# A norm by tokens and value tiles ahead of the convolution at the beginning, and the stick-breaking stage in a new order

## The chip, the core and the metric

The kernel runs on one core of one Trainium2 chip. A core has TensorE (PE, matrix multiply, results go to eight banks of PSUM), VectorE (DVE), ScalarE (ACT), GpSimd (POOL) and SyncE (SP), each with its own instruction queue, worked off in order; they wait for each other by semaphores. The metric is the device time of one execution in microseconds (us). Before the change it is 1169.18 us, the median of three runs (1169.01 to 1170.82).

## What is computed

Two transformer blocks on x of 256 tokens by 1024 features, in float32. The change touches only the mixer of the first block:

```python
h = rms_norm(x, norm_mix_g[l])
p = h @ w_in[l]
q = rms_norm(p[..., :s1].reshape(bsz, L, SB_HEADS, SB_HEAD_DIM), sb_q_norm_g[l])
k = rms_norm(p[..., s1:s2].reshape(bsz, L, SB_HEADS, SB_HEAD_DIM), sb_k_norm_g[l])
v = p[..., s2:s3].reshape(bsz, L, SB_HEADS, SB_HEAD_DIM)
o_sb = stick_breaking_attention(q, k, v)
o_conv = conformer_conv(p[..., s3:s4], ...)     # 31 taps, layer norm, silu, 256x256 matrix
o_ssm = s5_ssm(p[..., s4:], ...)                # 16 groups, 64 complex states, gated output
mixed = jnp.concatenate([rms_norm(o_sb, ...), rms_norm(o_conv, ...), rms_norm(o_ssm, ...)], axis=-1)
x = x + mixed @ w_out[l]
hx = rms_norm(x, norm_xa_g[l])
hm = rms_norm(mem, norm_mem_g[l])
x = x + memory_cross_attention(hx, hm, ...)     # keys and values of mem: hm @ xa_wk, hm @ xa_wv
```

In stick-breaking attention (8 heads of 64) a weight is exp(log_sigmoid(z) + the sum of log_sigmoid(-z) over the keys that come later). Behind this come cross attention, a gated feed-forward layer, and a second block of two layers with three more attentions and two feed-forward layers; none of it is changed.

## The kernel before

**Tiles and pieces.** Activations lie with features on the 128 partitions: a tile is 128 features by 256 tokens, and x is eight of them (xT). Weights come in pieces of 1 MB (1024 rows by 256 columns) into three slots `raw`. Each piece is split in halves: ScalarE copies a half to `whi` in a rounded format, VectorE writes raw minus whi to `wlo` (`split`). Activations are split likewise (act_hi, act_lo; mem_hi, mem_lo in mem_pair). A projection tile is 24 matmuls, three for each of eight row blocks: whi by act_hi, whi by act_lo, wlo by act_hi (lines 2009 to 2011; 2074 to 2076 with tokens as output rows for values). A slot's next piece may be split once the tiles of the old one are done: `after(name, idx)` stands on ScalarE and VectorE where the splits are due, and SP loads a piece when the low parts of the slot's last one are written.

**Order.** All orders are written by hand, one program for each engine; `Plan` only numbers tiles, pieces, PSUM banks (a ring of four) and semaphore values. The order on TensorE: 16 transposes of x, 16 of mem, sums of squares of x by matmuls with ones (`norm_sums`), transposes of the row vectors (gains, convolution taps: `col`, `tap`), the two tiles u (input of the state-space branch), with the sums of squares of mem between them, cb and ca (gate and input of the convolution, two tiles each), then q and k in turn (four each) with `ssm_matrices` and the first `conv_taps` among them, value tiles v with `inputs_of(1)` and `conv_sum` among them, and the stick-breaking stage.

**Stick-breaking stage.** For each of 8 heads: `scores_of(h)` (one head ahead), ScalarE's `sb_log1p` (three steps), VectorE's `sb_softplus`, `sums_of(h)` (matmuls with a triangle), ScalarE's Exp, `values_of(h)`. Between them TensorE does the 16 tiles of cross attention's keys (xk) and values (xv), two for each head (`kv_tile`), and small work for the other branches (`side_work`). In heads 0 to 3 the state-space branch runs along: `inputs_of(s)` writes one pair of state inputs to PSUM, ScalarE copies it to SBUF (`bu_out`, line 924), VectorE works a quarter of the states (`state_quarter`, 13 operations), `outputs_of(q)` reads them. The norms of the three branches, ("branch", 1) of the convolution, ("branch", 2) of the state-space branch and ("branch", 0) of stick-breaking, come at the end, and then `branch_projection` with w_out.

The generic helper lines: 766 is ScalarE's split, 1360 VectorE's, 2080 a plain matmul, 1353 a VectorE product, 1371 the scaling by a norm, 790 squares, 835 and 837 the logarithm and exponential of a norm.

## Time and profile before

| | us |
|---|---|
| median of three runs | 1169.18 |
| the profiled execution | 1177.42 |
| its span | 1175.3 |
| TensorE, VectorE, ScalarE, GpSimd busy | 1118.8, 839.6, 618.3, 39.2 |
| x landed, first matmul of u | 7.7, 25.3 |
| end of the second u tile | 39.3 |
| first matmul of q, of v | 55.1, 100.2 |
| taps of the convolution, two parts | 78.3 to 85.4, 92.1 to 100.3 |
| first scores, first value tile of mem | 120.0, 193.2 |
| end of the last value tile of mem | 234.1 |
| first matmul of xq, behind w_out | 269.6 |

A page of the profile gives each engine's busy time and what ended its idle time; the queries on the trace give the same for any stretch.
### The profile page before, as it was taken

Reading aid. Unit: us, or ns where it says so; the run is one execution under the profiler, and the core shown is the slowest. Engines: PE = TensorE matmul, PEld = TensorE weight load, DVE = VectorE, ACT = ScalarE, POOL = GpSimd, SP = SyncE. Lnnn points to the kernel's source line nnn. Section 1 sums busy time; section 2 is a strip of 40 time slices with the busy share of each in tenths; the row PEclk is TensorE's granted clock in tenths of the full one; section 3 lists DMA queues with packets and bytes.
Section 4 is the critical chain, followed back from the end, with each engine's and each line's share of the span. In section 5 each row is a group of like instructions: output and inputs, shape, how many; then the busy total and the mean of one; then the engine's idle time right before and its main releaser. Section 6 shows DMA issues by size and latency. Waiting matters only on the chain.

```text
span 1175.3 us, 20129 instructions
## 1 busy us (share of the span) xinstructions
PE 1118.8 (95%) x7660; PEld 988.1 (84%) x7660; DVE 839.6 (71%) x1277; ACT 618.3 (53%) x1104; POOL 39.2 (3%) x41
## 2 busy tenths in 40 slices
PE   5899899989999999999999999999999999999997
PEld 4787678879998999999987698999998779888886
DVE  2785686246678787887556678787887877788885
ACT  4634344556555554556355555454556675455554
POOL 2000000001020000001000010000001001000000
PEclk8998889989999999999999999999999999999999
DMA  8342312325366765655531056665758235576661
GB/s 265 109 144 73 108 37 73 108 70 164 90 192 178 214 178 164 193 176 172 165 126 36 1 180 180 205 176 158 211 143 186 66 91 177 145 214 186 181 169 72
DMA packets 218431, 169.69 MB, mean 144 GB/s; under 512 B 20827, under 2 KB 208130, under 8 KB 218242
## 3 DMA queue, kind: packets, MB, share of 16 engines
q1 hardware_dynamic: 217106, 164.44, 48.0%
q0 software_dynamic: 640, 2.95, 0.7%
q10 hardware_dynamic: 624, 1.44, 0.4%
q8 instruction: 44, 0.72, 0.3%
q14 instruction: 17, 0.14, 0.0%
HBM read 167.76 MB, written 1.05 MB: 144 GB/s over the span
## 4 chain that ended last, share of the span: by engine, by line
PE 80%; DVE 9%; ACT 7%; issue 2%; SPq 1%; DMA 1%; POOLq 0%; POOL 0%; DVEq 0%; ACTq 0%
PE bank L2441 19%; PE bank L2080 17%; PE bank L2009 10%; PE bank L2443 10%; PE bank L2010 9%; PE bank L2011 9%; DVE wlo L1360 2%; DVE arena L1353 2%; PE bank L2074 2%; PE bank L2076 2%; PE bank L2075 2%; ACT whi L766 1%; SPq L691 1%; ACT arena L1303 1%; DVE wlo L1756 1%
## 5 line engine op out<-in xcount | busy, mean ns | idle before, releaser
L2441 PE MATMUL bank<-mem_pair,whi 128*128 128x512 f32 x1056 | 375.8, 399 | 0.7 <-DVE xT L1677 0.7
L2443 PE MATMUL bank<-mem_pair,wlo 128*128 128x256 f32 x1056 | 296.3, 281 | 0.0
L2441 PEld LDWEIGHTS bank<-mem_pair,whi 128*128 128x128 f32 x1056 | 198.5, 188 | 47.7 <-issue 0.9
L1360 DVE TENSOR_TENSOR wlo<-raw,whi 128x1024 fp32r<-128x1024 f32 (+3 forms) x137 | 161.5, 1223 | 97.2 <-ACT whi L766 96.2
L2009 PE MATMUL bank<-act_hi,whi 128*128 128x256 f32 (+1 forms) x744 | 216.5, 291 | 10.5 <-DVE act_lo L1379 4.7
L2010 PE MATMUL bank<-act_lo,whi 128*128 128x256 f32 (+1 forms) x744 | 212.9, 286 | 0.0
L2011 PE MATMUL bank<-act_hi,wlo 128*128 128x256 f32 (+1 forms) x744 | 212.8, 286 | 0.0
L1756 DVE TENSOR_TENSOR wlo<-raw,whi 128x1024 fp32r<-128x1024 f32 x177 | 208.9, 1221 | 5.3 <-ACT whi L1140 1.6
L2443 PEld LDWEIGHTS bank<-mem_pair,wlo 128*128 128x128 f32 x1056 | 199.5, 189 | 0.8
L1140 ACT ACTIVATE whi<-raw 128x1024 fp32r<-128x1024 f32 x180 | 179.7, 1045 | 0.3 <-PE bank L2080 0.3
L2009 PEld LDWEIGHTS bank<-act_hi,whi 128*128 128x128 f32 (+1 forms) x744 | 143.8, 193 | 20.5 <-issue 13.2
L1160 ACT ACTIVATE arena<-arena 128x256 f32<-128x256 f32 x66 | 27.6, 418 | 249.4 <-DVE arena L1353 249.4
L2010 PEld LDWEIGHTS bank<-act_lo,whi 128*128 128x128 f32 (+1 forms) x744 | 144.0, 193 | 0.8 <-issue 0.7
L2011 PEld LDWEIGHTS bank<-act_hi,wlo 128*128 128x128 f32 (+1 forms) x744 | 144.0, 194 | 0.0
L2080 PE MATMUL bank<-arena 32*32 32x256 f32 (+9 forms) x1052 | 132.8, 384 | 8.7 <-ACT arena L924 2.1
L766 ACT ACTIVATE whi<-raw 128x1024 fp32r<-128x1024 f32 (+3 forms) x134 | 129.2, 1018 | 18.1 <-PE bank L2011 18.1
L1786 DVE TENSOR_REDUCE arena<-bank 128x256 f32<-128x512 f32 x132 | 90.7, 687 | 64.9 <-PE bank L2443 64.9
L1353 DVE TENSOR_TENSOR arena<-arena 128x256 f32<-128x256 f32 (+5 forms) x190 | 95.3, 503 | 40.5 <-ACT arena L1164 21.3
L2080 PEld LDWEIGHTS bank<-arena 32*32 32x32 f32 (+5 forms) x1052 | 81.6, 135 | 45.0 <-issue 14.9
L2009 PE MATMUL bank<-mem_pair,whi 128*128 128x256 f32 (+1 forms) x352 | 107.5, 305 | 2.1 <-DVE mem_pair L1670 2.1
L2010 PE MATMUL bank<-mem_pair,whi 128*128 128x256 f32 (+1 forms) x352 | 101.8, 289 | 0.0
L2011 PE MATMUL bank<-mem_pair,wlo 128*128 128x256 f32 (+1 forms) x352 | 101.5, 288 | 0.0
(221 smaller groups left out, 1442.9 us busy)
## 6 DMA issues: line engine op xcount, KB each, us to landing
raw<-in_ffn_w_in_dram SPq DMA_DIRECT2D x132, 512.0 KB, 5.2
raw<-in_ffn_w_out_dram SPq DMA_DIRECT2D x33, 1024.0 KB, 5.1
raw<-in_w_in_ab_dram SPq DMA_DIRECT2D x11, 1024.0 KB, 6.2
raw<-in_w_in_dram SPq DMA_DIRECT2D x9, 1024.0 KB, 7.0
raw<-in_xa_wk_dram SPq DMA_DIRECT2D x4, 1024.0 KB, 5.5
raw<-in_xa_wv_dram SPq DMA_DIRECT2D x4, 1024.0 KB, 5.0
raw<-in_w_out_dram SPq DMA_DIRECT2D x4, 1024.0 KB, 5.1
raw<-in_xa_wq_dram SPq DMA_DIRECT2D x4, 1024.0 KB, 5.1
```

The costliest lines, as they stand in the source:

```text
L766: act.activation(whi[g % SLOTS][:, h * n:h * n + n], raw[g % SLOTS][:, h * n:h * n + n], ACT.Copy)\
L1140: act.activation(whi[slot][:, h * 1024:h * 1024 + 1024], raw[slot][:, h * 1024:h * 1024 + 1024], ACT.Copy).then_inc(s_split_hi, 1)
L1353: return dve.tensor_tensor(dst, a, b, ALU.mult)
L1360: dve.tensor_tensor(wlo[g % SLOTS][:, at_], raw[g % SLOTS][:, at_], whi[g % SLOTS][:, at_].bitcast(F32), ALU.subtract).then_inc(s_split_lo, 1)
L1756: dve.tensor_tensor(wlo[slot][:, at_], raw[slot][:, at_], whi[slot][:, at_].bitcast(F32), ALU.subtract)\
L1786: dve.tensor_reduce(x[:, j, :], bank[2 * j + g][:].rearrange("p (h t) -> p t h", h=2), AX.X, ALU.add)\
L2009: pe.matmul(dst, w[0], a[0], start=start, stop=False, **kw)
L2010: pe.matmul(dst, w[0], a[1], start=False, stop=False, **kw)
L2011: return pe.matmul(dst, w[1], a[0], start=False, stop=stop, **kw)
L2080: return pe.matmul(dst, w, a, start=start, stop=stop, skip_group_check=True)
L2441: pe.matmul(b[:].rearrange("p (h t) -> p h t", h=2), w[0][:, k, g, :], mem_pair[:, :, k, :], start=k == 0, stop=False, skip_group_check=True)
L2443: last = pe.matmul(b[:, 0:T], w[1][:, k, g, :], mem_hi[:, k, :], start=False, stop=k == KC - 1, skip_group_check=True)
```

## The change

**Beginning.** The norm of x and of mem is taken token by token before the transposes. x lands in two halves (128 tokens each, tokens on partitions); ScalarE squares a half with a running sum for each token (`token_scale`), takes Ln and Exp of two columns, and ScalarE and VectorE scale one half each. TensorE transposes the scaled tokens, and ScalarE (`normed_high`) and VectorE (`normed_low`) write the high and low parts straight from PSUM with the gain. x is also transposed unscaled, for the residual; VectorE copies it out (`raw_out`). The gain of this norm and the 128x128 identity get loads of their own. The two u tiles are computed together, row block by row block. The three first weight pieces go to SP's queue before the row vectors, and mem is loaded by GpSimd, once piece u has landed. `token_transposes` of mem stand behind tile (cb, 1) and behind ca. 16 ones-matmuls go, 17 transposes come.

**q, k, v and the convolution.** All value tiles stand ahead of `conv_taps(0)`, and the taps, inputs_of(0), inputs_of(1) and conv_sum stand in one block before the first scores. VectorE's qk_norm, coefficients and rotations are spread anew to fit.

**Stick-breaking stage.** Scores run two heads ahead. softplus(0) stands inside the first state quarter. On TensorE outputs_of(h) stands between the two inputs of the next states, with scores_of(h + 2) ahead of both. ScalarE's splits are moved behind a head's weights, half by half (`kv_split`). The norm of the convolution and of the state-space branch is a slot earlier each; the squares of the stick-breaking outputs come in three parts, the last straight from PSUM, and the first four tiles of w_out take their conv rows, then their state-space rows, then the stick-breaking rows.

TensorE at the start of the program, before: x_landed and mem_landed are the two loads, ones the matrix of the sums.

```order
L2119 MATMUL bank<-cst,arena 128x128 [waits x_landed,consts_landed]
L2119 MATMUL bank<-cst,arena 128x128 x15
L2126 MATMUL bank<-cst,arena 128x128 [waits mem_landed]
L2126 MATMUL bank<-cst,arena 128x128 x15
L2080 MATMUL bank<-sq,ones 128x256 [waits squares_ready,transposes_evacuated,pool_step]
L2080 MATMUL bank<-sq,ones 128x256
L2080 MATMUL bank<-sq,ones 128x256 [waits squares_ready]
L2080 MATMUL bank<-sq,ones 128x256
L2080 MATMUL bank<-sq,ones 128x256 [waits squares_ready]
```

The same place after, up to the first row block of u (x_scaled lies in hf and sq, the unscaled x in arena):

```order
L2208 MATMUL bank<-cst,arena 128x8 [waits mix_gain_landed,identity_landed]
L2212 MATMUL bank<-cst,arena 128x128 [waits x_landed0]
L2212 MATMUL bank<-cst,arena 128x128 x7
L2212 MATMUL bank<-cst,arena 128x128 [waits x_landed1]
L2212 MATMUL bank<-cst,arena 128x128 x7
L2202 MATMUL bank<-cst,hf 128x128 [waits tokens_scaled1,tokens_scaled0,transposes_evacuated]
L2202 MATMUL bank<-cst,sq 128x128
L2202 MATMUL bank<-cst,hf 128x128
L2202 MATMUL bank<-cst,sq 128x128
```

mem and the sums of squares are gone from the head of TensorE's queue. ScalarE after, from the last high copies of x's norm to the copies of col and tap:

```order
L873 ACTIVATE act_hi<-bank,mix_gain 128x256 x4
L783 ACTIVATE whi<-raw 128x1024 x4
L860 ACTIVATE rms,tok_sums<-arena 128x1024
L860 ACTIVATE arena,tok_sums<-arena 128x1024
L863 ACTIVATE tok_scale<-tok_sums,eps 128x2
L866 ACTIVATE tok_scale<-tok_scale 128x2
L910 ACTIVATE arena<-arena,tok_scale 128x1024
L798 ACTIVATE arena<-bank 128x256 x2
L783 ACTIVATE whi<-raw 128x1024 x2
L914 ACTIVATE col<-bank 128x109
L915 ACTIVATE tap<-bank 128x62
L918 ACTIVATE arena<-log_dt 64x8 x2
```

In before the same queue had col and tap ahead of the first high copies:

```order
L766 ACTIVATE whi<-raw 128x1024 x2
L835 ACTIVATE rms<-bank,eps 128x256
L837 ACTIVATE rms<-rms 128x256
L869 ACTIVATE col<-bank 128x109
L870 ACTIVATE tap<-bank 128x62
L844 ACTIVATE act_hi<-hf 128x512 x4
L766 ACTIVATE whi<-raw 128x1024 x4
L790 ACTIVATE sq<-bank 128x512 x4
```

So col and tap moved behind the splits of three pieces, mem's squares and u's evacuation; TensorE's tile (cb, 1) waits for them as before.

TensorE behind the values of head 1 up to the first key tile of head 2, before (sq,ones is the squares' sum, 32x256 outputs, 128x256 inputs and scores):

```order
L2080 MATMUL bank<-sq,ones 128x256 [waits rms_ready,squares_ready,bu_evacuated]
L2080 MATMUL bank<-sq,ones 128x256
L2080 MATMUL bank<-arena 32x256 [waits sb_out_evacuated,states_ready]
L2080 MATMUL bank<-arena 32x256 x7
L2080 MATMUL bank<-arena 128x256 [waits bu_evacuated,rms_ready]
L2080 MATMUL bank<-arena 128x256
L2080 MATMUL bank<-arena 128x256 [waits bu_evacuated]
L2080 MATMUL bank<-arena 128x256
L2080 MATMUL bank<-arena 128x256 [waits sb_weights,tile_evacuated_dve]
L2080 MATMUL bank<-arena 128x128
L2080 MATMUL bank<-cst 128x128 x2
```

After:

```order
L2161 MATMUL bank<-sq,ones 128x256 [waits rms_ready,squares_ready,bu_evacuated]
L2161 MATMUL bank<-sq,ones 128x256
L2161 MATMUL bank<-arena 128x256 [waits sb_weights,tile_evacuated_dve]
L2161 MATMUL bank<-arena 128x128
L2161 MATMUL bank<-cst 128x128 x2
L2161 MATMUL bank<-arena 128x256 [waits bu_evacuated,rms_ready]
L2161 MATMUL bank<-arena 128x256
L2161 MATMUL bank<-arena 32x256 [waits sb_out_evacuated,states_ready]
L2161 MATMUL bank<-arena 32x256 x7
L2161 MATMUL bank<-arena 128x256 [waits bu_evacuated]
L2161 MATMUL bank<-arena 128x256
```

The scores stand first now, and the outputs between the two inputs.

The core of the diff:

```diff
-    sp.dma_start(x_tok, ins["x"][0].rearrange("(t p) d -> p t d", p=P)).then_inc(s_x, 16)
-    load(pieces[0])
-    for name, k in VECTORS:
+    for t in range(TT):
+        sp.dma_start(x_tok[:, t, :], ins["x"][0, t * P:t * P + P, :]).then_inc(s_x[t], 16)
+    for g in range(SLOTS):
+        load(pieces[g])
+    for name, k in VECTORS[1:]:
...
+    pool.wait_ge(s_landed[0], 16)
+    pool.dma_start(m_tok, ins["mem"][0].rearrange("(t p) d -> p t d", p=P)).then_inc(s_mem, 16)
...
+    def token_scale(which, tok, landed):
+        for t in range(TT):
+            act.wait_ge(*landed[t])
+            act.activation((rms, v_sb)[t].rearrange("p a n -> p (a n)"), tok[:, t, :], ACT.Square,
+                           accum_out=tok_sums[:, which, t:t + 1]).then_inc(s_toksq, 1)
+        act.wait_ge(s_toksq, 2 * which + 2)
+        act.activation(tok_scale[:, which, :], tok_sums[:, which, :], ACT.Ln, scale=1.0 / D, bias=eps[:, 0:1])\
+           .then_inc(s_tokln, 1)
+        act.wait_ge(s_tokln, which + 1)
+        act.activation(tok_scale[:, which, :], tok_scale[:, which, :], ACT.Exp, scale=-0.5).then_inc(s_tokr, 1)
+        act.wait_ge(s_tokr, which + 1)
+    def normed_high(which, c):
+        hi, gain = (act_hi, mem_hi)[which], (mix_gain, col[:, ROW["norm_mem_g"]:ROW["norm_mem_g"] + KC])[which]
+        act.wait_ge(s_tr, (TR_X, TR_MEM)[which] + c + 1)
+        act.activation(hi[:, c, :], bank[4 + c % 4][:, (c // 4) * T:(c // 4) * T + T], ACT.Copy,
+                       scale=gain[:, c:c + 1]).then_inc(s_nhi, 1)
...
+    act.activation(mix_gain[:], bank[4][:, 0:KC], ACT.Copy).then_inc(s_trev, 1)
+    token_scale(0, x_tok, [(s_x[t], 16) for t in range(TT)])
+    act.activation(sq.rearrange("p a n -> p (a n)"), x_tok[:, 1, :], ACT.Copy, scale=tok_scale[:, 0, 1:2])\
+       .then_inc(s_tok[1], 1)
+    act.wait_ge(s_trev, 1)
+    for h in range(2):
+        split(0, h)
+        for c in range(4 * h, 4 * h + 4):
+            normed_high(0, c)
...
+    token_scale(1, m_tok, [(s_mem, 16)] * TT)
+    act.activation(m_tok[:, 1, :], m_tok[:, 1, :], ACT.Copy, scale=tok_scale[:, 1, 1:2]).then_inc(s_tok[1], 1)
+    for i in range(2):
+        evacuate("u", i, u[:, i, :])
+    act.wait_ge(s_tr, TR_ROWS + 1)
+    act.activation(col[:], bank[3][:, 0:ROWS], ACT.Copy).then_inc(s_trev, 1)
+    act.activation(tap[:], bank[3][:, T:T + 62], ACT.Copy).then_inc(s_trev, 1)
...
+    for h in range(4):
+        kv_tile(2 * h)
+        sb_weights(h)
+        kv_tile(2 * h + 1)
+        kv_split(h, 0)
+        if h % 2:
+            sb_out(h)
+        rms_of(("xk", h), bank[4][:, 0:T], 256)
+        kv_split(h, 1)
+        if h < 3:
+            bu_out(2 * h + 2)
+        sb_log1p(h + 2)
+        if h < 3:
+            bu_out(2 * h + 3)
...
+    sb_weights(7)
+    branch_high(0)
+    squares(("branch", 0), 1, o_sb[:, 2, :], T)
+    branch_high(1)
+    kv_tile(15)
+    act.wait_ge(s_sbo, 8)
+    squares(("branch", 0), 2, bank[7][:, 0:T], T)
+    sb_out(7)
+    rms_of(("branch", 0), bank[4][:, 0:T], 512)
+    kv_split(7, 0)
+    branch_high(2)
+    branch_high(3)
+    kv_split(7, 1)
...
+    raw_out(0)
+    raw_out(1)
+    dve.wait_ge(s_tokr, 1)
+    dve.tensor_scalar(hf.rearrange("p a n -> p (a n)"), x_tok[:, 0, :], tok_scale[:, 0, 0:1], None, ALU.mult)\
+       .then_inc(s_tok[0], 1)
+    for h in range(2):
+        split(0, h)
+        for c in range(4 * h, 4 * h + 4):
+            normed_low(0, c)
+    raw_out(2)
+    raw_out(3)
...
+    state_quarter(0, lambda: sb_softplus(0))
+    sb_softplus(1)
...
+    pe.wait_ge(s_raw, 2)
+    for c in range(KC):
+        if c % 4 == 0:
+            pe.wait_ge(s_split_lo, split_value(0, c // 4))
+        pe.wait_ge(s_nlo, c + 1)
+        w = [x[:, c, :] for x in weights(("w_in", "u", 0))]
+        for i in range(2):
+            last = three(ring_bank("u", i)[:, 0:T], [x[:, P * i:P * i + P] for x in w],
+                         (act_hi[:, c, :], act_lo[:, c, :]), c == 0, c == KC - 1)
+            if c == KC - 1:
+                last.then_inc(tile_done, 1)
+        if c < 4:
+            token_transposes(x_scaled, 0, (c + 4,))
...
         project("k", j, ("w_in", "k", j // 2), P * (j % 2))
-        if j == 1:
-            ssm_matrices()
-        if j >= 2:
-            conv_taps(j - 2)
-        if j == 3:
-            inputs_of(0)
     for i in range(4):
         project_tokens("v", i, ("w_in", "v", i // 2), i % 2)
         if i == 0:
             sum_squares(("qk", 3), 0, bank[4][:], 2, True, True, blocks)
-            inputs_of(1)
-            conv_sum()
+        if i == 1:
+            ssm_matrices()
+    conv_taps(0)
+    conv_taps(1)
+    inputs_of(0)
+    inputs_of(1)
+    conv_sum()
...
+    scores_of(1)
+    pe.wait_ge(s_nlo, 2 * KC)
     for h in range(8):
-        if h < 7:
-            scores_of(h + 1)
-        if h == 0:
-            pe.wait_ge(s_h, HF["norm", 1] + 4)
         kv_tile(2 * h)
         side_work(h, SLOT_A)
         sums_of(h)
...
             if h:
                 pe.wait_ge(s_bu_ev, 2 * h + 2)
             sum_squares(("xk", h), 0, bank[4][:, 0:T], 2, True, True)
-            outputs_of(h)
+        if h < 6:
+            scores_of(h + 2)
         if h < 3:
             pe.wait_ge(s_rms, 2 * stat_no["xk", h] + 1)
             inputs_of(2 * h + 2)
+        if h < 4:
+            outputs_of(h)
+        if h < 3:
             inputs_of(2 * h + 3)
-    sum_squares(("branch", 2), 0, bank[4][:, 0:T], 2, True, True)
-    pe.wait_ge(s_sbev, 4)
-    sum_squares(("branch", 0), 0, bank[7][:, 0:T], 2, True, False)
-    sum_squares(("branch", 0), 1, bank[7][:, 0:T], 2, False, True)
+    sum_squares(("branch", 0), 0, bank[4][:, 0:T], 2, True, False)
+    sum_squares(("branch", 0), 1, bank[4][:, 0:T], 1, False, False)
...
+        for m0, parts in ((0, ((4, 5), (6, 7), (0, 1, 2, 3))), (4, ((4, 5, 6, 7, 0, 1, 2, 3),))):
+            for part, order in enumerate(parts):
                 for m in range(m0, m0 + 4):
                     b = claim("w_out", m, ("w_out", m // 2)) if part == 0 else ring_bank("w_out", m)
                     w = [x[:, :, P * (m % 2):P * (m % 2) + P] for x in weights(("w_out", m // 2))]
-                    for i, k in enumerate(order):
-                        if m == 0 and i % 2 == 0:
-                            pe.wait_ge(s_h, HF["branch", 0] + 2 * part + i // 2 + 1)
+                    for k in order:
+                        if m == 0 and k % 2 == 0:
+                            pe.wait_ge(s_h, HF["branch", 0] + (2 + k // 2 if k < 4 else k // 2 - 2) + 1)
                         last = three(b[:, 0:T], [x[:, k, :] for x in w], [x[:, k, :] for x in hi_lo],
-                                     part == 0 and i == 0, part == 1 and i == 3)
-                    if part:
+                                     k == 4, k == 3)
+                    if part == len(parts) - 1:
                         last.then_inc(tile_done, 1)
+                    if m == 0 and part == 0:
+                        sum_squares(("branch", 0), 2, bank[4][:, 0:T], 1, False, True)
```

## Rows read from the trace of the kernel before

**Rows 1.** The page: busy time and share of the span, by engine.

```profile
PE 1118.8 (95%) x7660; PEld 988.1 (84%) x7660; DVE 839.6 (71%) x1277; ACT 618.3 (53%) x1104; POOL 39.2 (3%) x41
```

**Rows 2.** Six stages: stretch, length, busy us (instructions) by engine, PEclk, DMA, GB/s.

```profile
0.00:25.30 25.30, 11.15 (x50) 9.38 (x50) 4.70 (x8) 10.38 (x17) 6.24 (x15) 0.91 0.91 280
25.30:55.10 29.80, 24.08 (x161) 22.71 (x161) 22.59 (x54) 17.83 (x31) 0.00 (x0) 0.90 0.41 131
55.10:120.00 64.90, 61.58 (x810) 53.08 (x810) 45.21 (x69) 26.74 (x43) 0.00 (x0) 0.92 0.32 102
120.00:193.10 73.10, 64.29 (x384) 52.07 (x384) 53.95 (x78) 29.61 (x54) 0.00 (x0) 0.88 0.21 70
193.10:234.00 40.90, 39.45 (x280) 36.16 (x279) 12.95 (x19) 20.75 (x38) 0.00 (x0) 1.00 0.31 103
234.00:270.00 36.00, 31.49 (x217) 29.42 (x216) 19.27 (x32) 18.02 (x31) 2.60 (x2) 0.91 0.26 86
```

**Rows 3.** TensorE's waits, 0 to 270 us: us in total, times, longest.

```profile
PE bank L2080 <- DVE arena L1578: 5.0, 1, 5.0
...
PE bank L2009 <- DVE act_lo L1379: 4.7, 2, 2.9
PE bank L2009 <- ACT arena L908: 4.3, 1, 4.3
PE bank L2080 <- ACT arena L924: 2.1, 3, 0.7
```

**Rows 4.** Timeline of the beginning: start, us, engine, line, operation.

```profile
7.71 3.41 PE L2119 MATMUL bank<-cst,arena 128*128 128x128 f32 x16 [7.71 <-DMA arena<-in_x_dram]
...
21.96 0.32 PE L2133 MATMUL bank<-cst,arena 109*128 109x109 f32 x1 [1.70 <-DMA arena<-in_ssm_lam_im_dram]
...
25.34 0.55 PE L2009 MATMUL bank<-act_hi,whi 128*128 128x256 f32 x1 [2.87 <-DVE act_lo L1379]
```

**Rows 5.** DMA issues, 0 to 60 us: KB each, us from issue to landing.

```profile
arena<-in_x_dram SPq DMA_DIRECT2D x1, 1024.0 KB, 6.8
...
arena<-in_ssm_glu_w_dram POOLq DMA_DIRECT2D x1, 512.0 KB, 8.8
```

**Rows 6.** Tile raw, 0 to 2 us: the load of the first weight piece.

```profile
DMA to landing us min/median/max: 16.0/16.0/16.0
```

**Rows 7.** Timeline of ScalarE: two high copies of a weight piece.

```profile
39.74 2.01 ACT L766 ACTIVATE whi<-raw 128x1024 fp32r<-128x1024 f32 x2
```

**Rows 8.** Timeline of VectorE: four low parts of weights, four scaled mem tiles.

```profile
29.27 4.63 DVE L1360 TENSOR_TENSOR wlo<-raw,whi 128x1024 fp32r<-128x1024 f32 x4 [0.25 <-ACT whi L766]
...
45.58 1.65 DVE L1371 SCALAR_TENSOR_TENSOR hf<-bank,col,rms 128x256 f32<-128x256 f32 x4
```

**Rows 9.** Four stretches, columns as in rows 2.

```profile
130.00:140.00 10.00, 9.06 (x44) 7.83 (x46) 2.25 (x4) 2.75 (x5) 0.00 (x0) 0.66 0.32 107
140.00:170.00 30.00, 27.75 (x158) 22.52 (x155) 22.13 (x33) 11.12 (x23) 0.00 (x0) 0.83 0.21 71
145.00:150.00 5.00, 5.00 (x22) 4.60 (x21) 4.57 (x7) 1.74 (x4) 0.00 (x0) 0.50 0.15 54
250.00:260.00 10.00, 10.00 (x86) 10.00 (x85) 3.40 (x5) 3.44 (x5) 0.00 (x0) 1.00 0.00 0
```

**Rows 10.** Timelines of TensorE and VectorE, one head of the stick-breaking stage.

```profile
174.35 2.98 PE L2080 MATMUL bank<-arena 128*32 128x256 f32 x20
...
179.80 1.42 DVE L1353 TENSOR_TENSOR arena<-arena 128x512 f32<-128x512 f32 x2 [2.53 <-ACT arena L924]
...
189.98 0.84 PE L2080 MATMUL bank<-arena 128*32 128x256 f32 x6 [0.88 <-DVE arena L1353]
```

**Rows 11.** Timeline of TensorE behind the last value tile.

```profile
237.75 1.13 PE L2080 MATMUL bank<-sq,ones 128*128 128x256 f32 x4 [2.04 <-ACT sq L790]
...
245.66 0.39 PE L2009 MATMUL bank<-act_hi,whi 128*128 128x256 f32 x1 [1.82 <-DVE act_lo L1379]
```

456 lines of the change are left out of this document (226 added, 230 removed).

## The prediction

> **What bounds the kernel now.** I read the page's totals first, then TensorE's waits, then a table by stages, then the timelines of the stages where the waits sit. TensorE is busy 95% of the span and VectorE 71% [rows 1], so a gain can only come from where TensorE stands still or runs at the lower of its two clock levels. The table by stages covers the part that the change touches, up to 270 us, where the first tile of the next projection begins; after it nothing is changed [rows 2]. There TensorE is busy 11.2 of 25.3, 24.1 of 29.8, 61.6 of 64.9, 64.3 of 73.1, 39.5 of 40.9 and 31.5 of 36.0 us: 38.0 us idle in all. The granted clocks of the same rows (0.91, 0.90, 0.92, 0.88, 1.00, 0.91) are means over 1.0 and 0.5, the levels of 2.4 and 1.2 GHz. Length times what is missing to 1.0 is the time lost: 2.3 + 3.0 + 5.2 + 8.8 + 0 + 3.2 = 22.5 us. So 60.5 us of these 270 are not matmul work at full rate. The longest waits: 7.7 for x [rows 4], and [rows 3] 5.0 on softplus (L1578), 4.7 on the low halves act_lo, 4.3 on the sigmoid's exponential (L908), 2.1 on the state inputs' copies (L924).
>
> **Beginning: from the start to the first q tile (before: 55.1 us).** In before, x lands at 7.7; all transposes of x and mem, squares, ones-matmuls and the row vectors (wait until 21.96 for ssm_lam_im) come ahead of the first projection, at 25.34, and it starts at half rate [rows 4]. After: x comes in two halves, alone at the head of its queue, the identity apart. The old x took 6.8 us to land with the constants beside it [rows 5]; I put the first half at 5.2 and the second at 6.7. Sixteen transposes took 3.41 us [rows 4], so they end near 8.7. ScalarE's squares (1024 columns, 1.0 us each by the weight copies [rows 7]), Ln, Exp and the scaled copy end near 9.8; eight scaled transposes follow, half of 3.41, 1.7 us. Piece u now travels right behind x, so not 16.0 us after issue [rows 6] but at about 10. Copy to whi 1.0, low part 1.2 [rows 7, 8], first low activation 0.4 (four in 1.65 [rows 8]): u's matmuls begin at 12.6. 48 matmuls and four pairs of transposes take 5.8 + 0.9 us at full rate (86 matmul records in 10 us near 250 [rows 9], a few missing, so 0.12 each and 2.9 a tile); the first half of them at half rate makes it end near 20.5. In before both u tiles were done at about 39.
>
> Then comes the new wait. Tile (cb, 1) needs col and tap, and on ScalarE these stand behind the four copies of pieces cb and ca (3.9), two squares of mem (2.1), Ln and Exp (0.5), one scaled copy (1.05), two evacuations (0.66), two copies of the q piece (2.0) and themselves (0.45): 10.7 us behind the last high activation, at about 18, plus some 1.3 for landings: 30. Tile (cb, 0) runs 22.6 to 25.5, so TensorE waits about 4.6 us here, and such a wait (5.0 us, before the sums of head 0) left it at half rate for most of the next 10 us (0.66 [rows 9]: 3.4 us lost), here I take 1.7 us. Then cb1 and the two ca tiles, 8.9, and sixteen mem transposes at full rate, half of 3.41 or 1.8, plus the 1.7: q starts at 42.5 to 43 instead of 55.1. The half-rate slice at 55 goes too. **Term A: -13.5.** Bounds: -5, if the third piece or mem lands 6 us later and pushes ScalarE's whole row of work; -17 without the wait. VectorE's chain (low halves, 5.5 us of phase arithmetic, low activations) ends near 50, ahead of q1's statistics; ScalarE is back from its two table loads at 49, just before it is needed at 51.
>
> **Value tiles ahead of the convolution.** No matmul goes or comes; the order changes, so that the 15 us of taps and the state inputs come last and what VectorE prepares for them (diagonals, matrices, rotations) has 15 us more. The 65 us held 3.3 idle and 5.2 of lost clock [rows 2]. The rotations, six operations of 1.2 us a half, end near 97 in my count, when the taps end: a tie. I take -5 and leave the rest for a half-rate slice where TensorE hangs on ScalarE's copies between the last tap and the first scores. **Term B: -5**, bounds +2 and -8.5.
>
> **Head 0 of the stick-breaking stage.** In before softplus(0) stood on VectorE behind the whole first state quarter (13 operations, 10.2 us) and two low halves; TensorE waited 5.0 us [rows 3] and lost 3.4 us of clock after it [rows 9]. Now it stands after the quarter's fifth operation, 3.6 us in, and TensorE has two score groups and a tile (5.8 us) to do. Covered by 1.5 us. **Term C: -8.4**, bounds -4 (another wait of a few us) and -8.4.
>
> **Heads 1 to 3.** One head from outputs to outputs is 174.35 to 189.98, 15.6 us [rows 10], with a wait for a copy of the state inputs (2.1 in three [rows 3], 0.7 each) and 0.88 for the states. Now scores and outputs lie between the two state inputs, so the copy is hidden. But the loop outputs, second input, copy, ten us of states, outputs is a closed one: 2.1 + 0.9 + 0.7 + 10.15 (179.80 to 189.95, its first two operations and the release of the outputs stand in [rows 10]) = 13.9, beside TensorE's own work of 14.07. A tie again; from 15.6 to 14.3 three times. **Term D: -4**, bounds 0 and -9 (the half rate between 140 and 170, clock 0.83, 5.1 us lost [rows 9], gone too). I keep it.
>
> **Tail, after the last value tile.** Before: 1.45 us idle in the fifth stage and 4.5 in the sixth, 2.04 and 1.82 of these before the branch sums and before the stick-breaking rows [rows 11], as the norms of three branches follow each other, and 3.2 us of lost clock [rows 2]: 9.2 together. After: two norms are done before tile 15, the squares of the last pair are split off, and 48 matmuls on the conv and ssm rows (5.8 us) stand between the last squares and the first use of the stick-breaking rows, whose chain I make 0.4 + 0.4 + 0.8 + 0.9 + 1.0 + 0.6 + 0.7 = 4.8 us. Covered. **Term E: -9**, bounds -5 and -9.2.
>
> **Sum.** -13.5 - 5 - 8.4 - 4 - 9 = -39.9. Nearly every term assumes that the next item is ready with 0 to 1.5 us to spare in four places (rotations, states, q and k norms twice), and each miss costs a wait and perhaps a half-rate slice of 1.7 us. I add 4.9 for these: -35. The profiled execution took 1177.4 us, 2.1 more than its span, and 8.2 more than the median 1169.2; the sum is a difference of two executions of one kind, so it is taken from the median: 1134.
>
> **A rule against the sum.** Half rate stands at 145 to 150 us, where TensorE is busy 5.00 of 5.00 us [rows 9] and the longest wait shortly before is 0.7 us. The Trainium skill (TensorE: Matmul & The Clock Gate, HAM oscillation) has the clock fall at pauses for data. By that rule, with the long waits gone, the half rate of heads 1 to 3 would go as well, and the sum would be 5 us better; the row speaks against it, and I go by the row.
>
> **Rivals.** (1) *The beginning shifts its bound to ScalarE.* Its list behind u has no gap, so any late landing goes straight to cb1. For it: in before the first piece needed 16.0 us against 6.8 for x of the same size [rows 5, 6], since 4 KB rows of mem went beside 1 KB rows of weights; now three pieces, mem and the small tensors still share the engines. Price: A -7.5, D -1, two more half-rate slices: -22, 1147. (2) *All waits and all half-rate slices go:* A -15, B -8, C -8.4, D -6, E -9: -46.4, less a rest of 1.4: -45, 1124. Against it: half rate without long waits [rows 9]. (3) *Only one of the two parts pays,* the other being eaten by a VectorE chain (rotations late by 7 us in front of the state copies): -12, 1157. (4) *Slower.* mem is now asked for by GpSimd, only after piece u. The largest transfer that GpSimd issued in before, 512 KB, landed 8.8 us after its issue [rows 5]. ScalarE and TensorE stand behind it. Everything else pays some 35 us, so mem would have to be usable at 18 + 35 = 53 us or later instead of 18 to have the kernel no faster; at 60 it would be 7 us slower, 1176. Nothing in the trace is near it. (5) The waits are replaced one for one: no change.
>
> The Trainium skill (DMA: Bandwidth & Descriptors, Queues, rings and completion order) says that each engine takes turns between queue rows by whole packets; by it mem, in long rows, takes more than its share beside the third piece, in short ones. The 16.0 us of the first piece agree [rows 6]; what it does here is the condition of rival 1.
>
> **Chances.** Forecast 45%, rival 1 25%, rival 2 18%, rival 3 7%, no change 2%, rival 4 3%. The forecast alone spans 1128 to 1141. The range for 8 in 10 reaches to rival 2 and most of rival 1: 1121 to 1152. 0.2% is 2.3 us, about what a measurement tells from nothing: faster 95%, same 2%, slower 3%.
>
> **What would show it.** Right: u's matmuls from about 12 to 21 us; one wait of 3 to 6 us before cb1, released by ScalarE's tap; q0 near 43; first scores near 101; no wait over 1 us on softplus; heads 14 to 14.5 us apart, half rate at one or two places among them; w_out from the last value tile on without a wait over 1 us; the first tile of the next projection near 232 instead of 269.6. Wrong: first u matmuls after 18 us, a wait of ScalarE on mem over 3 us, waits of TensorE on rotations or states of several us, or half-rate slices summing over 15 us.

## The result

The changed kernel takes 1133.1 us (median of four executions, 1132.4 to 1134.0) against 1170.0 for the kernel before (1169.0 to 1179.0). The ratio is 0.967, 95% interval 0.962 to 0.972. 1134 was predicted, with 1121 to 1152 as the range. In the profiled executions the span went from 1175.3 to 1130.9 us. These 44.4 us are more than the 36.9 between the medians, and the difference turns out to be the instructive part of this case.

The page after: busy time and share of the span, answering to [rows 1].

```profile
PE 1098.0 (97%) x7645; PEld 971.9 (86%) x7645; DVE 837.4 (74%) x1275; ACT 619.0 (55%) x1112; POOL 40.1 (4%) x42
```

All of TensorE's waits after, from the start to the first tile of the next projection at 224.95 us (us in total, times, longest), answering to [rows 3].

```profile
PE bank L2208 <- DMA cst<-consts_dram: 6.2, 1, 6.2
PE bank L2238 <- DMA arena<-in_ssm_lam_im_dram: 3.7, 1, 3.7
PE bank L2090 <- DVE act_lo L1459: 1.5, 1, 1.5
PE bank L2161 <- issue: 1.2, 1, 1.2
PE bank L2202 <- DVE hf L1471: 0.8, 1, 0.8
PE bank L2161 <- DVE arena L1420: 0.7, 1, 0.7
```

The reader is to see that softplus, the sigmoid, the copies of the state inputs and the squares have all gone from the list. What is left is the landing of the identity (x is no longer the last to land), one wait of 3.7 us for the row vectors, and four short ones.

Timeline of TensorE after, at the ends of the stages (start, us, engine, line, operation, idle time before it), answering to [rows 4, 10]: first transpose, first matmul of u, row vectors, first q tile, state inputs, first scores, last head with states, first tile of the value projection on mem, first tile of the next projection.

```profile
6.18 0.27 PE L2208 MATMUL bank<-cst,arena 8*128 8x8 f32 x1 [6.18 <-DMA cst<-consts_dram]
...
14.28 0.55 PE L2090 MATMUL bank<-act_hi,whi 128*128 128x256 f32 x1 [1.48 <-DVE act_lo L1459]
...
26.70 0.41 PE L2238 MATMUL bank<-cst,arena 109*128 109x109 f32 x1 [3.75 <-DMA arena<-in_ssm_lam_im_dram]
...
42.64 0.36 PE L2090 MATMUL bank<-act_hi,whi 128*128 128x256 f32 x1
...
96.42 2.87 PE L2161 MATMUL bank<-arena 32*32 32x256 f32 x28 [1.22 <-issue]
...
100.28 0.48 PE L2161 MATMUL bank<-arena 64*128 64x256 f32 x1
...
156.34 1.92 PE L2161 MATMUL bank<-arena 128*32 128x256 f32 x16 [0.70 <-DVE arena L1420]
158.19 0.39 PE L2155 MATMUL bank<-whi,mem_pair 128*128 128x256 f32 x1
...
224.95 0.28 PE L2090 MATMUL bank<-mem_pair,whi 128*128 128x256 f32 x1
```

The same stages by busy time, after (columns as in [rows 2]); the last row is the stretch behind the wait for the row vectors.

```profile
0.00:42.64 42.64, 30.42 (x196) 29.18 (x196) 22.29 (x40) 27.39 (x51) 7.12 (x16) 0.92 0.82 260
42.64:100.28 57.64, 56.42 (x814) 48.73 (x812) 49.71 (x90) 29.42 (x48) 0.00 (x0) 1.00 0.44 145
100.28:158.19 57.91, 57.21 (x385) 45.50 (x384) 51.90 (x76) 29.82 (x56) 0.00 (x0) 1.00 0.17 56
158.19:224.95 66.76, 66.76 (x491) 62.47 (x489) 32.46 (x52) 37.38 (x67) 2.59 (x2) 1.00 0.33 107
25.00:32.00 7.00, 5.30 (x24) 5.02 (x25) 4.68 (x5) 6.22 (x15) 0.00 (x0) 0.51 1.07 343
```

From 158.19 us on TensorE is busy 66.76 of 66.76 us. The clock is 1.00 (2.4 GHz) in three of four stages; the 0.92 of the first is the one stretch at 25 to 32 us at half rate (1.2 GHz). By its length it costs 3.4 us, and 2.6 of these while TensorE worked (busy 5.30 of 7.00 us), as it began inside the wait of 3.7. The rest of the program, 906 us from there, took the same time in both profiled executions.

```profile
14.28:18.30 4.02, 4.02 (x19) 4.02 (x20) 2.65 (x5) 1.30 (x3) 3.39 (x6) 1.00 1.07 372
18.42:22.96 4.54, 4.54 (x39) 4.33 (x37) 3.29 (x6) 3.43 (x6) 0.00 (x0) 1.00 1.06 260
```

19 matmuls in 4.0 us and 39 in 4.5: TensorE is at half rate up to 18.3 us. In the kernel before the record begins at 10.7 us, in its second profiled execution (below) at 16.8. So a clock row of the first stage is not to be compared between executions, and the mean clock of a whole execution is a little too high by an amount that varies.

### The profile page after: what moved, and what is told of

It reads as the page before. It is cut to its first block, busy times and chain, and to the rows that moved or that the text cites. A ratio compares the mean times of both kernels' runs of the same rounds, so it can differ in the third digit from the quotient of the medians.

```text
span 1130.9 us, 20116 instructions
## 1 busy us (share of the span) xinstructions
PE 1098.0 (97%) x7645; PEld 971.9 (86%) x7645; DVE 837.4 (74%) x1275; ACT 619.0 (55%) x1112; POOL 40.1 (4%) x42
## 4 chain that ended last, share of the span: by engine, by line
PE 86%; DVE 5%; ACT 5%; SPq 1%; issue 1%; DMA 1%; POOLq 0%; POOL 0%; DVEq 0%; ACTq 0%
PE bank L2542 20%; PE bank L2161 18%; PE bank L2090 11%; PE bank L2092 10%; PE bank L2091 10%; PE bank L2544 10%; PE bank L2155 2%; PE bank L2156 2%; PE bank L2157 2%; DVE wlo L1427 1%; DVE arena L1420 1%; ACT arena L1370 1%; DVE wlo L1837 1%; SPq L702 1%; DMA arena<-in_ssm_lam_im_dram 1%
## 5 line engine op out<-in xcount | busy, mean ns | idle before, releaser
L2092 PEld LDWEIGHTS bank<-act_hi,wlo 128*128 128x128 f32 (+1 forms) x744 | 143.2, 192 | 0.0
L1420 DVE TENSOR_TENSOR arena<-arena 128x256 f32<-128x256 f32 (+5 forms) x190 | 95.4, 504 | 32.7 <-ACT arena L1231 21.3
L2090 PE MATMUL bank<-mem_pair,whi 128*128 128x256 f32 (+1 forms) x352 | 105.1, 299 | 2.2 <-DVE mem_pair L1751 2.2
L2091 PE MATMUL bank<-mem_pair,whi 128*128 128x256 f32 (+1 forms) x352 | 99.5, 283 | 0.0
```

What stands on the lines that cost most here:

```text
L1420: return dve.tensor_tensor(dst, a, b, ALU.mult)
L2090: pe.matmul(dst, w[0], a[0], start=start, stop=False, **kw)
L2091: pe.matmul(dst, w[0], a[1], start=False, stop=False, **kw)
L2092: return pe.matmul(dst, w[1], a[0], start=False, stop=stop, **kw)
```

## The experiments

Twelve runs were made, in four groups, two of them repeats of before and after. The medians of the kernel before in the four groups were 1170.8, 1172.2, 1172.1 and 1172.1 us, and 1169.3 in the first experiment, since its executions spread over 10 us; so the kernels are compared with each other by their own medians, and the ratio to before stands beside where it matters.

**1. The kernel before, again.** No edit.

> The kernel before, once more. In the trace of before the span was 1175.3 us at a mean granted clock of 0.979, and its time 1177.4, 8.2 above the median of the other runs; the changed kernel's profiled execution agreed with its own median (1132.8 and 1133.1). Theory A (the clock makes the difference: in an ordinary run of before some of the half-rate slices of the trace are missing): runs of 1169 to 1171 us show a mean clock near 0.986, since 8.2 us of 1175 at half rate less is 0.007; runs near 1178 show 0.979; and a trace taken in a run of 1170 us lacks half rate at 140 to 170 us, where the trace of before lost 5.1 us, and part of another slice. Theory B (recording itself slows before): every recorded span is near 1175 us, whatever the clock.

Twelve executions: median 1169.3, from 1169.1 to 1176.0 us. Theory A held. The times of this kernel stand in steps, and the longer ones go with a lower clock (time, mean granted clock over the span; seven of the executions of before in this group):

```
1169.15  0.987      1174.45  0.982      1177.5   0.979
1170.78  0.987      1175.76  0.982      1179.01  0.979
1172.39  0.985
```

The profiled execution this time took 1169.2 us, span 1167.1. Its stages, cut at the same events as those of the changed kernel (first q tile, first scores, first value tile on mem, first tile of the next projection):

```profile
0.00:55.07 55.07, 35.38 (x210) 32.37 (x211) 27.29 (x61) 28.21 (x48) 6.24 (x15) 0.93 0.65 199
55.07:117.17 62.10, 59.40 (x811) 52.05 (x811) 45.24 (x69) 26.77 (x43) 0.00 (x0) 0.95 0.33 106
117.17:188.18 71.01, 62.19 (x386) 50.36 (x385) 54.56 (x79) 29.62 (x54) 0.00 (x0) 0.90 0.23 75
188.18:261.51 73.33, 67.60 (x492) 62.26 (x490) 31.05 (x48) 38.79 (x69) 2.41 (x2) 1.00 0.29 95
```

TensorE waits as in the first trace of before (5.0 for softplus, 4.3 for the sigmoid; idle 36.9 us up to here and 38.0 there), but the clock's records hold only 13.6 us lost up to here, and 22.2 in the first. The first stage tells nothing of this: its record starts later here, and it is 55.1 us long in both. From the first q tile on the three stages are 206.4 us long and 214.5 in the first trace. Of these 8.1 us, 0.9 are idle time and 7.2 are clock (9.9 us lost for 17.1): half rate is missing at 239 to 250 us, and there is less of it from 140 to 170. The same program, the same waits, another 8.1 us: this is the 8.2 us by which the first profiled execution lay above the median. Which stretches of this program fall to half rate is not the same from one execution to the next.

The mean clock orders the times of this kernel, but not of every one. The beginning alone (experiment 2) took 1152.4 us at a mean clock of 0.983 and 1155.2 at 0.988, softplus(0) put back (experiment 3) 1138.1 at 0.989 and 1139.6 at 0.994. Only one execution of each was traced, so why is not shown.

**2. Each part alone.** The diffs are the two halves of the change: the beginning with value tiles ahead of the convolution, and the order of heads and tail. (Where they meet, the sum of squares of the stick-breaking branch has two groups in the first and three in the second.)

> Only the new beginning (norm by tokens, value tiles ahead of the convolution); the stick-breaking stage in its old order. Theory A (the two parts add, each by the terms of the prediction): -18.5 us (A -13.5, B -5), 1151. By the distances in the two traces it would be -19.8 (first q tile 55.1 to 42.6, first scores another 7.3 earlier), 1150. Rival (only the stick-breaking stage pays, since the rotations of VectorE now stand late, in front of the old order's first state quarter): -10 or less. The wait before the sums of head 0 should be back, 4 to 6 us, with half rate behind it.

> Only the new order of the stick-breaking stage; the old beginning. Theory A (prediction's terms C, D, E, -8.4 -4 -9): -21.4, 1148. Theory B (by the traces, where these stretches became 24.9 us shorter, less the 8.2 us by which the profiled run of before lay above its median, if those 8.2 lay in this stage): -16.7, 1153. Rival: -25 or more, if the two parts get in each other's way in the changed kernel, so that each alone gives more than its share of the 37. Heads 0 to 3 should stand 14.0 to 14.5 us apart with no wait over 1 us, and no half rate between 120 and 234 us if half rate only follows waits.

The beginning alone: 1154.0 us (1149.8 to 1155.3), 16.8 below before's 1170.8, ratio 0.983. The stick-breaking stage alone: 1150.9 (1149.5 to 1153.9), 19.9 below, ratio 0.981. Together 36.7; from the same 1170.8 the whole change gives 37.7 (36.9 from the 1170.0 of its own group). So the parts add to 1 us, or to 2.5 if the 1169.3 of experiment 1 is taken for before, and each lies near its terms (-18.5 and -21.4). Both pay, so the rival in which one eats the other is out.

One detail was not as expected. With the beginning alone, the wait for softplus(0) did not come back. TensorE ran at half rate from 98 to 109 us, through the scores and the first key tile:

```profile
98.00:109.00 11.00, 11.00 (x37) 7.88 (x36) 8.95 (x13) 5.09 (x10) 0.00 (x0) 0.53 0.01 1
```

It arrived at the sums at 110.3 us, and softplus(0) had just ended at 110.2. A slow stretch had taken the place of the wait. In the kernel with the new stick-breaking order alone there is no wait but one of 0.7 us from 117 to 234 us, and no half rate in it.

**3. Softplus(0), in before and in the changed kernel.** First the edit in before:

```
-            state_quarter(0)
+            state_quarter(0, lambda: sb_softplus(0))
...
-            sb_softplus(0)
```

> The kernel before, with one edit: softplus(0) stands behind the fifth operation of the first state quarter instead of behind the whole quarter. Theory A (term C): the wait of 5.0 us before the sums of head 0 goes, and the half rate directly behind it (3.4 us): -8.4, 1161. Theory B (half rate at 140 to 170 us is an after-effect of the same wait): the trace loses these 5.1 us as well, and against a profiled run of before -13.5; against ordinary runs, if those lack the half rate at 140 to 170, -5 to -8. Theory C (half rate at 145 to 150 us has nothing to do with that wait): the trace still shows a slice at half rate between 140 and 170 us.

1167.0 us (1164.4 to 1170.0), ratio 0.995, interval 0.993 to 0.997: 2.3 us below the twelve executions of experiment 1 (the two spans, 1164.8 and 1167.1, give the same), and not 8.4. The wait of 5.0 is gone. The heads give 0.9 of it back: a further wait for the exponential of the weights (L1030), perhaps as the loop of states now bounds them. And the clock gives nothing: 13.7 us lost as before. Half rate moved from 126 to 133 us to 133 to 140, where the waits ahead are short, and a stretch at 235 to 239 us makes the tail 1.5 us longer than in experiment 1:

```profile
120.00:133.00 13.00, 12.31 (x86) 9.55 (x84) 12.04 (x17) 6.58 (x13) 0.00 (x0) 1.00 0.14 43
133.00:140.00 7.00, 7.00 (x31) 6.59 (x31) 6.50 (x11) 2.14 (x4) 0.00 (x0) 0.51 0.67 222
```

Theory C: the half rate of the heads does not need the long wait. Then the same thing undone in the changed kernel:

```
-            state_quarter(0, lambda: sb_softplus(0))
+            state_quarter(0)
+            sb_softplus(0)
```

> The changed kernel with one edit undone: softplus(0) again behind the whole first state quarter. By the trace of the changed kernel the quarter then ends near 110.0 us, and TensorE stands ready for the sums of head 0 at 106.0: a wait of 4.5 us. Theory A (a pause of 5 us is what brings the half rate, term C): +4.5 and 3.4 us of half rate behind it, +7.9, 1141. Theory B (the half rate of before hangs on the many short waits, one or two of 0.7 to 0.9 us in each head, not on the one long wait; the previous run, in which this wait alone was taken from before, lost 13.7 us of clock as before did, 13.6): +4.5 and no half rate between 100 and 225 us, 1137.5. Rival (VectorE's loop of states gives the wait back in the later heads): +2 or less.

1138.7 us (1137.2 to 1139.9), 5.6 above the changed kernel. The timeline of TensorE and the stretch around it:

```profile
109.89 0.79 PE L2162 MATMUL bank<-arena,cst 128*128 128x256 f32 x1 [4.47 <-DVE arena L1650]
```

```profile
109.00:113.00 4.00, 3.11 (x13) 2.93 (x14) 1.30 (x3) 0.49 (x1) 0.00 (x0) 0.57 0.00 0
113.00:225.00 112.00, 111.30 (x778) 95.81 (x777) 70.32 (x104) 60.60 (x109) 1.30 (x1) 1.00 0.25 85
```

The 4.5 us are as worked out from the trace, and 1.7 us of clock go with them, half of Theory A's 3.4 and not the nothing of Theory B; behind them none. So this edit is worth 5.6 us in the changed kernel and 2 to 4 in before: what a wait costs depends on what stands around it.

**4. The order inside heads 0 to 2, undone.**

```
-                sb_log1p(h + 2)
-                if h < 3:
                     bu_out(2 * h + 3)
+                sb_log1p(h + 2)
...
-                if h < 6:
-                    scores_of(h + 2)
-                if h < 3:
-                    pe.wait_ge(s_rms, 2 * stat_no["xk", h] + 1)
-                    inputs_of(2 * h + 2)
                 if h < 4:
...
                 if h < 3:
+                    pe.wait_ge(s_rms, 2 * stat_no["xk", h] + 1)
+                    inputs_of(2 * h + 2)
                     inputs_of(2 * h + 3)
+                if h < 6:
+                    scores_of(h + 2)
```

> The changed kernel with the order inside heads 0 to 2 as before: outputs, both state inputs, then scores, and on ScalarE the two copies of the state inputs one behind the other, ahead of the scores' log1p. Theory A (term D, -4): the wait for the copy comes back, 0.7 us in each of three heads, and 0.9 for the states or the scores: heads 15.6 instead of 14.1 us apart, +4 to +5, 1137.5. Theory B (half rate follows such repeated short waits): besides, half rate at one to three places between 110 and 170 us, 1.7 to 5 us, so +6 to +10, 1141. Rival (no difference, since VectorE's loop of states bounds the heads in either order): +1 or less.

1139.3 us (1137.3 to 1141.8), 6.2 above the changed kernel. Rows of TensorE's timeline, then the stretches between:

```profile
115.19 0.48 PE L2160 MATMUL bank<-arena 32*128 32x256 f32 x1 [0.69 <-ACT arena L953]
...
131.42 0.69 PE L2160 MATMUL bank<-arena 32*128 32x256 f32 x2 [0.69 <-ACT arena L953]
...
147.61 0.69 PE L2160 MATMUL bank<-arena 32*128 32x256 f32 x2 [0.69 <-ACT arena L953]
```

```profile
116.00:120.00 4.00, 4.00 (x17) 3.35 (x16) 2.88 (x5) 1.68 (x4) 0.00 (x0) 0.57 0.73 257
120.00:133.00 13.00, 12.31 (x83) 9.51 (x82) 10.80 (x16) 5.79 (x11) 0.00 (x0) 1.00 0.06 20
133.00:137.00 4.00, 4.00 (x21) 3.87 (x20) 3.62 (x6) 1.72 (x4) 0.00 (x0) 0.57 0.59 202
```

The three waits of 0.69 us are back, and behind two of them TensorE runs at half rate while it is busy 4.00 of 4.00 us, 3.4 us lost in this execution. So Theory B. Idle time grew by 2.3 us (the 0.9 for the states stands where the changed kernel has 0.7), the clock's loss by 3.4. These 5.7 are more than this execution shows: at 1137.3 us it is the fastest of the six and 4.5 above the profiled one of the changed kernel, so not all of the half rate turned into time. The other five have a mean clock of 0.988 to 0.992 for its 0.993; they were not traced.

The other four traces with the old order bear it out. With this one they are five; each has the wait of 0.69 us three times, and in each half rate begins behind two of the three (us):

```
                    waits of 0.69 end at      half rate begins at
before              143.2   161.8   178.0     143.9   164.3   -
before, again       139.7   155.3   171.5     -       156.7   173.8
softplus(0) only    131.9   150.6   166.2     133.0   -       167.2
beginning only      119.7   136.9   153.0     122.3   139.3   -
this kernel         115.2   131.4   147.6     116.5   133.6   -
```

In the changed kernel and the stick-breaking stage alone, which have none of these waits, the heads run at full rate throughout. One rival was not told apart: the edit that brings the waits back also puts the same small matmuls in another order.

**5. The convolution ahead of the value tiles again.** TensorE and ScalarE as in before; on VectorE the matrices and both rotations stand ahead of the last q and k norm, since that norm waits for a sum that stands behind the taps here.

> The changed kernel with the convolution's taps and the first state inputs ahead of the value tiles again; VectorE makes the matrices and both rotations ahead of the last q and k norm, which the old order needs. Term B says that value tiles ahead of the convolution are worth 5 us: +5, 1138. Theory of slack: in the changed kernel VectorE has 2.4 us of diagonals at 68.4 to 70.7 us, the copies of the matrices at 76.7 to 77.9 and the rotations until 97.0; pulled ahead of the taps they make TensorE wait for the copies of the matrices, and the last q and k norm comes late: +4 to +8. Rival: the order of these stages is worth nothing once the beginning is shorter: within 1 us.

1147.0 us (1146.9 to 1147.9): 13.9 slower. VectorE's copy of the turned matrices was 7.25 us late. Since that could be my place for the copy, one more kernel had it two weight halves earlier:

```
-            after("q", 3)
-            after("k", 3)
             dve.wait_ge(s_bcT, 1)
...
+            after("q", 3)
+            after("k", 3)
```

> The earlier kernel with the convolution ahead of the value tiles, with one edit: VectorE copies the turned matrices ahead of the low parts of two weight halves and not behind. In that run TensorE waited 7.2 us for these copies, at 76 us, and lost 3.4 us of clock behind it, and the kernel was 13.9 us slower than the changed one. Theory A (VectorE's diagonals, until 70.7 us, are what bounds the old order now, whatever the order of the copies): a wait of 3 to 4 us stays, 1142 to 1144. Rival (the 14 us were mostly the place of these copies): at most 1138, the 5 us of term B.

1144.4 us (1144.0 to 1145.3), 11.3 slower. The row in each:

```profile
75.95 0.68 PE L2161 MATMUL bank<-arena 32*32 32x256 f32 x8 [7.25 <-DVE arena L1603]
```

```profile
72.20 0.67 PE L2161 MATMUL bank<-arena 32*32 32x256 f32 x16 [2.70 <-DVE arena L1601]
```

A wait of 2.7 us stays, and further back 1.9 for the convolution's partial sum, which before had too (at 106 us), and 1.9 for softplus, besides 5.1 us of clock between 72 and 104 us. So against these two old orders the value tiles' new place is worth 11 to 14 us behind the new beginning, and not the 5 of term B. The likely reason, not tested by itself: the beginning makes TensorE come 12 us earlier, and VectorE, busy 49.7 of 57.6 us of the stage, has to be given that time elsewhere. What the best old order would give was not tried, so these runs put no upper or lower limit on term B.

**6. The rows first.** The largest wait left that is not the start is the one for the row vectors. Their 25 loads stand in SP's queue behind the second and third weight piece. First edit:

```
-            for g in range(SLOTS):
-                load(pieces[g])
+            load(pieces[0])
             for name, k in VECTORS[1:]:
...
-            for name in pieces[SLOTS:]:
+            for name in pieces[1:]:
```

and the copies of col and tap ahead of mem's squares on ScalarE.

> The changed kernel with the small row vectors asked for directly behind the first weight piece, ahead of the second and third, and the copies of col and tap on ScalarE ahead of mem's squares. In the changed kernel TensorE waits 3.7 us for these rows (until 26.7) and then runs at half rate until 31.9 (3.4 us lost). Low parts of the second piece are done at 24.6, so the wait shrinks to 1.6. Theory A: -2.1 of wait and -3.4 of clock, -5.5, 1127.5. Rival 1 (VectorE's rotations, which end at 97.0 us, and its other work up to there take the gain back): -1 to -2. Rival 2 (the half rate comes anyway behind a wait of 1.6 us): -2. Rival 3 (27 small loads ahead of the second piece push its landing by more than 2 us): 0 or slower.

1132.1 us (1131.8 to 1137.0), 0.9 faster than the changed kernel. ScalarE's timeline shows why not 5.5:

```profile
26.81 2.00 ACT L782 ACTIVATE whi<-raw 128x1024 fp32r<-128x1024 f32 x2 [5.23 <-DMA raw<-in_w_in_dram]
28.72 0.24 ACT L909 ACTIVATE col<-bank 128x109 f32<-128x109 f32 x1
28.86 0.21 ACT L910 ACTIVATE tap<-bank 128x62 f32<-128x62 f32 x1
```

SP took 8.2 us to issue the small loads, the third piece landed at 26.8 (in the changed kernel its copies began by 22.5 without a wait), and col and tap stand behind its copies: three waits (1.4, 2.3 and 0.8) for the one of 3.7. The clock held at 1.00 through them; its one stretch at half rate came earlier, at 13.7 to 17.1 us. Second edit, which puts col, tap and mem's squares ahead of the third piece:

```
-            for g in range(1, SLOTS):
-                split(g, 0)
-                split(g, 1)
+            split(1, 0)
+            split(1, 1)
+            act.wait_ge(s_tr, TR_ROWS + 1)
+            act.activation(col[:], bank[3][:, 0:ROWS], ACT.Copy).then_inc(s_trev, 1)
+            act.activation(tap[:], bank[3][:, T:T + 62], ACT.Copy).then_inc(s_trev, 1)
...
             token_scale(1, m_tok, [(s_mem, 16)] * TT)
...
+            split(2, 0)
+            split(2, 1)
```

and the low parts on VectorE in the same order.

> The previous edit (small row vectors asked for behind the first weight piece) with another order on ScalarE and VectorE: in that run ScalarE waited 5.2 us for the third piece, which landed at 26.8 us, with col, tap and mem's squares queued behind it, and TensorE stood 2.3 us for tap and 0.8 for mem. Now the copies of the second piece, col, tap, mem's squares, scales and scaled copy come ahead of those of the third piece. Theory A (that queue is what held it): no wait for tap, tile (cb, 1) directly behind (cb, 0), the q tiles start at 37 to 38 us instead of 40.7, and the kernel is 3 us faster than that run and 4 faster than the changed kernel: 1129. Rival 1 (VectorE's rotations, state inputs' copies and the statistics of q and k are late instead): within 1 us of that run, 1131 to 1132, with new waits behind q0. Rival 2 (the third piece is now the last, low parts at 30): q tiles from 39, 1131.

The mechanism was right and the gain did not come: 1133.5 us (1128.4 to 1134.7). The q tiles start at 38.0 us and the state inputs at 92.4 instead of 96.4. Then:

```profile
92.43 0.45 PE L2162 MATMUL bank<-arena 32*32 32x256 f32 x8 [1.16 <-issue]
```

```profile
94.00:105.00 11.00, 11.00 (x35) 7.63 (x34) 6.05 (x10) 5.24 (x11) 0.00 (x0) 0.53 0.01 1
```

The 4.0 us gained were paid back at half rate, 5.1 us (the first key tile starts at 103.0 us, and at 103.1 in the changed kernel), in a stretch where TensorE is busy all the time: state inputs, scores and the first key tile, behind 14 us of taps. Neither theory nor rivals named this place. Of six executions one escaped, at 1128.4 us.

**7. A full tile behind the taps.** The kernel of the run before, with the last value tile moved:

```
-            for i in range(4):
+            for i in range(3):
                 project_tokens("v", i, ("w_in", "v", i // 2), i % 2)
...
             conv_taps(1)
+            project_tokens("v", 3, ("w_in", "v", 1), 1)
             inputs_of(0)
```

with its copy on ScalarE behind that of the partial sum, and the weight halves that it frees behind log1p(1) and softplus(1).

> The kernel of the run before (small row vectors first), with the last value tile (24 full matmuls, 2.9 us) moved between the convolution's taps and the first state inputs; both rotations then stand ahead of that tile's end, and the copies and low parts of the two weight halves that it frees go behind the log1p of heads 0 and 1. In that run the state inputs came 4.3 us earlier than in the changed kernel (92.4 against 96.8), but 5.1 us of clock were lost at 94 to 105 us, where taps, a pause of 1.2 us, state inputs, scores and other small matmuls follow each other, and its median was no better (1133.5); one execution of six took 1128.4. Theory A (half rate hangs on that long stretch of small matmuls with the pause in it, and a full tile in its middle breaks it): no half rate from 90 to 110 us in most executions, median 1128.5 to 1130. Theory B (half rate comes with the pause of 1.2 us and the small state inputs and scores behind it, wherever the tile stands): unchanged, 1133 to 1134. Rival (the weight halves freed later make a later tile wait): over 1135.

1128.7 us, 1128.5 to 1129.2: all six executions in 0.7 us. Ratio to before 0.963 (0.9605 to 0.965).

```profile
82.88 0.40 PE L2164 MATMUL bank<-arena 32*32 32x256 f32 x2 [1.20 <-issue]
```

```profile
82.00:110.00 28.00, 26.93 (x377) 22.85 (x379) 22.25 (x27) 11.80 (x22) 0.00 (x0) 1.00 0.01 2
```

No half rate behind 17 us. No work was removed; a tile of 24 full matmuls stands between the small ones. The pause for which the trace names no releaser also moved, into the taps. Theory A had the time; since the pause moved too, the run does not tell whether the tile or the pause's place did it. This kernel beats both, by 4.4 us the changed one.

**8. The changed kernel, again.** No edit.

> The changed kernel once more, as the reference for the small differences of the other runs: 1132.5 to 1133.5, with 1.7 to 3.4 us of lost clock ahead of 35 us and none behind, if its half rate hangs on the pause of 3.7 us at 23 to 27 us alone; another execution of before lost 13.6 us of clock and not 22.2, at other places.

1133.1 us, five of six within 1132.8 to 1133.2 and one at 1136.8 with a clock of 0.990 instead of 0.996. The trace lost 3.4 us, at 24 to 32 us. Before's executions spread over 10 us, this one's over 4, and those of experiment 7 over 0.7. Fewer waits are not the whole of it: the first kernel of experiment 5, with a wait of 7.25 us and two of 1.9, spread over 1.0.

## Why the prediction was right, point by point

Stage lengths in us against two profiled executions of before: the ordinary one of experiment 1, and the first, by [rows 2] with a last stage that ends at 269.6:

```
                         before,      before,     after   predicted   got (ordinary / first)
                         ordinary     first run
to the first q tile      55.1         55.1        42.6    A  -13.5    -12.4 / -12.5
to the first scores      62.1         64.9        57.6    B   -5.0     -4.5 /  -7.3
heads 0 to 3             71.0         73.1        57.9    C+D -12.4   -13.1 / -15.2
value tiles and tail     73.3         76.5        66.8    E   -9.0     -6.6 /  -9.7
sum                                                           -39.9   -36.6 / -44.7
```

(By [rows 2] the third stage begins 0.04 us earlier than the scores, hence 44.7 for 44.6.)

- **A** was right in size, to 1.1 us, and in the q tile's time (42.6 for 42.5 to 43). About 1 us of the 13.5 was for the half rate behind 55 us (55.1 to 58.5 in the first trace), which the table has in the next stage. Its inside was not right: u began at 14.3 and not 12.6, ended at 23.0 and not 20.5, and the one wait stood in front of the row vectors, for a DMA, and not in front of tile (cb, 1) for ScalarE's tap. I had the rows landed in time. They stood behind three weight pieces in SP's queue: SP came to the first at 6.8 us, needed 4.5 us to issue it, and issued the last at 18.6; TensorE had them at 26.7. Behind them there was no wait for tap: what I had priced as 4.6 came as 3.7 further ahead. Its clock cost was 2.6 behind the wait (3.4 by length) and not 1.7. The 22.5 us of clock that I counted in before leave out the half rate ahead of 10.7 us, as the rows do.
- **B** held in the ordinary comparison. The tie that I saw in the rotations was none: they ended at 97.0 us, and the state inputs' first copy, for which they must be done, came at 98.6.
- **C**: the wait went, but half of its priced clock loss (3.4) was not its own. Undone it costs 5.6 us, of 8.4; taken alone in before it gave 2.3 to 3.8.
- **D** was too small. The heads stand 14.1 us apart (key tiles at 103.1, 117.2, 131.3 and 145.4), for 14.3 in the sum. What I left out is the clock: undone, D costs 6.2 us and not 4, and half rate comes back behind the 0.7 us waits. I had gone by the row 145 to 150 [rows 9], half rate at 5.00 of 5.00 us busy, against the Trainium skill (TensorE: Matmul & The Clock Gate, HAM oscillation), which has the clock fall at pauses for data. The row was read rightly and concluded from wrongly: half rate shows behind the waits, and a fully busy stretch says nothing on what stood ahead of it. The row's own stretch began at 143.9 us, behind a wait of 0.69 that ended at 143.2, and experiment 4 shows it busy 4.00 of 4.00 us behind such a wait. By the rule the heads' half rate had to go, and it went. Yet the rule speaks of waits for a DMA that are several times as long, and it alone would not have named 94 to 105 us in experiment 6, where the only pause was 1.2 us.
- **E** in size by the first execution; in the ordinary one the 3.2 us of clock in it were not there, and -6.6 remain. TensorE's tail is without any wait, as forecast. E was not undone by itself.
- **The allowance of 4.9** was for misses in four places. There was one, 0.7 us for the states.
- **From the profiled execution to the median.** This is the step that failed in the working. I noted that the profiled execution stood 8.2 us above the median and took the sum from the median all the same, as "a difference of two executions of one kind". They were not of one kind: 7.2 of the 22.5 us of clock that I counted, 3.4 of them in the tail, were in that execution only, and nothing can win them in the median. The terms had left part of the clock out on another ground (3.5 of the 8.5 us of idle time and clock in B's stage, and the 5.1 of the heads in D), and came to -39.9, where the two traces give -44.7 and the medians -36.9: 3.0 too much. The allowance of 4.9, made for another reason, took off 1.9 more than that, and with a base of 1169.2 for 1170.0 the forecast ends 0.9 from the result. What repeats is the idle time: it fell by 23.8 us against the first execution of before and by 22.8 against the ordinary one. The clock lost from the first q tile on fell by 17.1 and by 9.9. That the forecast came within 1 us is two errors of unlike sign, and luck.
- **Rivals.** ScalarE as the bound of the beginning: near at hand, ScalarE is busy 27.4 of 42.6 us, but no landing went through it. All waits and all half rate gone: true in substance (3.4 us of recorded clock and 14.1 of idle time left, of 22.5 and 38.0, besides the half rate ahead of 18.3 us), and still not 1124, as before did not have as much to lose. mem by GpSimd's queue landed 9.1 us after its issue, at about the 8.8 that I took, and ScalarE had it at 24.3 at the latest.

## What to carry to other kernels

## What was not expected of the hardware

- The times of one program stand in steps (1169.2, 1170.8, 1172.4, 1174.5, 1175.8, 1177.5, 1179.0 us), with the mean clock from 0.987 to 0.979, at waits that are the same in the two traces (1177.4 and 1169.2 us).
- Half rate for 10 us on end (94.6 to 104.8; the row 94 to 105 has clock 0.53) with TensorE busy 11.00 of 11.00 us, after no pause longer than 1.2 us.
- SP needs 8.2 us to issue 25 loads of 0.2 to 8 KB, 0.33 each, and the weight pieces behind them are asked for that much later.
- A pause of 1.1 to 1.25 us of TensorE with no releaser in the trace, once in eight of the ten traces with the new beginning, ending at 95.4 to 96.8, 92.4 or 82.9 us; in the two of experiment 5 it is 0.8 us and missing. In all nine traces that have it, a transfer of 16 KB on the queue that the profile calls instruction lands 0.0 to 0.7 us before the pause begins; in the changed kernel (window 94 to 97 us) it runs from 94.2 to 95.1, and TensorE stands from 95.2 to 96.4:

```profile
q8 instruction: 1, 0.02, 2.0%
```

So a wait for instructions is a candidate. It was not tested, and most such transfers have no pause behind them.
